# Banded attention of layer 1: the scaling of the probabilities on GpSimd, the results out of PSUM on VectorE

## What is computed

```python
def swa_sink_attention(q, k, v, sinks):
    ...
    s = jnp.einsum('bnqkgd,bnskd->bnkgqs', qc, kb).astype(F32) * (dh ** -0.5)
    s = jnp.where(valid[None, :, None, None, None, :], s, -jnp.inf)
    sink = jnp.broadcast_to(sinks.astype(F32).reshape(hk, grp)[None, None, :, :, None, None], s.shape[:-1] + (1,))
    p = jax.nn.softmax(jnp.concatenate([s, sink], axis=-1), axis=-1)[..., :-1]
    o = jnp.einsum('bnkgqs,bnskd->bnqkgd', p.astype(vb.dtype), vb)
```

## Time and profile before

| | |
|---|---|
| median of 3 runs | 2487.57 us (2487.36 to 2490.05) |
| profiled execution, first to last instruction | 2484.3 us |
| busy share TensorE, VectorE, ScalarE, GpSimd | 97%, 68%, 41%, 21% |
| the attention of layer 1 in it | 1681.4 to 1734.0 us |
| its 16 steps | about 3.0 us each |

### The profile page before, as it was taken

How to read it: one execution, slowest core, us unless ns; L and a number is a source line. 1 busy time by engine, 2 the same in 40 slices (tenths; PEclk the granted TensorE clock), 3 DMA queues, 4 the chain that set the end, 5 groups by cost and what they waited for, 6 DMA issues and landing times.

```text
span 2484.3 us, 33631 instructions
## 1 busy us (share of the span) xinstructions
PE 2417.9 (97%) x12846; PEld 1905.7 (77%) x12846; DVE 1688.6 (68%) x2659; ACT 1029.0 (41%) x1810; POOL 523.9 (21%) x485
## 2 busy tenths in 40 slices
PE   9999999998999999999999999998999999999998
PEld 6587778875556878888888886775878888888887
DVE  5389966855654698777765478728579777775557
ACT  5423324545444343333333344529344333333344
POOL 5025534320000023433341000000003433432000
PEclk9999989999999999999999999999999999999999
DMA  6121100010003425544568651110335544548663
GB/s 192 47 68 43 43 26 11 2 36 1 1 26 118 144 94 182 173 162 162 170 234 286 194 163 51 43 43 18 94 127 171 177 158 156 174 159 313 214 198 128
DMA packets 236271, 298.26 MB, mean 120 GB/s; under 512 B 13424, under 2 KB 175232, under 8 KB 227024
## 3 DMA queue, kind: packets, MB, share of 16 engines
q1 hardware_dynamic: 220848, 207.66, 27.1%
q0 software_dynamic: 15264, 88.45, 9.5%
HBM read 206.95 MB, written 88.60 MB: 119 GB/s over the span
## 4 chain that ended last, share of the span: by engine, by line
PE 89%; DVE 6%; ACT 3%; issue 2%; POOL 0%; DVEq 0%; ACTq 0%; POOLq 0%
PE ps L374 24%; PE ps L376 24%; PE ps L375 24%; PE ps L3084 3%; PE ps L3061 2%; PE ps L3072 1%; DVE met L2209 1%; PE ps L2448 1%; ACT d_p L1719 1%; PE ps L2462 1%; PE ps L2457 1%; PE ps L1991 1%; PE ps L2501 1%; PE ps L2425 1%; PE ps L2510 1%
## 5 line engine op out<-in xcount | busy, mean ns | idle before, releaser
L374 PE MATMUL ps<-uhi,whi 128*128 128x512 f32 x608 | 244.9, 403 | 7.9 <-DVE ulo L533 3.3
L374 PE MATMUL ps<-q_T,whi 128*128 128x512 f32 x640 | 249.2, 389 | 1.6 <-ACT upr L858 1.6
L376 PE MATMUL ps<-q_T,wlo 128*128 128x512 f32 x640 | 249.0, 389 | 0.0
L375 PE MATMUL ps<-q_T,whi 128*128 128x512 f32 x640 | 249.0, 389 | 0.0
L374 PE MATMUL ps<-q_B,whi 128*128 128x512 f32 x608 | 238.9, 393 | 2.4 <-DVE q_B L533 2.4
L374 PE MATMUL ps<-ahi,whi 128*128 128x512 f32 x616 | 240.4, 390 | 0.0
L376 PE MATMUL ps<-ahi,wlo 128*128 128x512 f32 x616 | 239.7, 389 | 0.0
L375 PE MATMUL ps<-alo,whi 128*128 128x512 f32 x616 | 239.7, 389 | 0.0
L375 PE MATMUL ps<-ulo,whi 128*128 128x512 f32 x608 | 237.0, 390 | 0.0
L376 PE MATMUL ps<-uhi,wlo 128*128 128x512 f32 x608 | 237.0, 390 | 0.0
L376 PE MATMUL ps<-q_B,wlo 128*128 128x512 f32 x608 | 236.7, 389 | 0.0
(11 more groups left out here) (474 smaller groups left out, 5161.6 us busy)
## 6 DMA issues: line engine op xcount, KB each, us to landing
wraw<-in_ffn_w_gate_dram SPq DMA_DIRECT2D x44, 512.0 KB, 5.2
wd<-in_ffn_w_down_dram POOLq DMA_DIRECT2D x22, 1024.0 KB, 7.2
w_sums<-wd POOLq DMA_DIRECT2D x22, 1024.0 KB, 5.1
wraw<-w_sums SPq DMA_DIRECT2D x40, 512.0 KB, 3.8
araw<-act_sums SPq DMA_DIRECT2D x40, 512.0 KB, 4.6
wraw<-in_ffn_w_down_dram SPq DMA_DIRECT2D x30, 512.0 KB, 5.9
araw<-acts SPq DMA_DIRECT2D x30, 512.0 KB, 6.0
wraw<-in_ab_w_in_dram SPq DMA_DIRECT2D x24, 512.0 KB, 3.8
```

Source lines behind the costliest of these rows:

```text
L374: nc.tensor.matmul(dst, wh, xh, start=start, stop=False, **kw)
L375: nc.tensor.matmul(dst, wh, xl, start=False, stop=False, **kw)
L376: return nc.tensor.matmul(dst, wl, xh, start=False, stop=stop, **kw)
```

## The change

In `norm`, the product of `d_p` with `d_inv` leaves VectorE. A new function `swa_pool`, called in GpSimd's list behind `d_prepare`, does the same product in the same place, and waits for the reciprocal (`d_den`) in each step. `result` leaves ScalarE: VectorE copies the 128x256 numbers out of PSUM, as the last piece of each step, behind `norm(n)`.

```diff
@@ swa_act
-            def result(n):
-                b, g = divmod(n, 2)
-                act.wait_ge(*after("d_out", n + 1))
-                act.activation(dq[:, 2 * g:2 * g + 2, b * P:(b + 1) * P],
-                               bank(6 + n % 2)[:, 0:256].rearrange("p (a n) -> p a n", a=2), ACT.Copy).then_inc(S("d_y"), 1)
-
             soft(0)
             for n in range(2 * NB):
                 if n + 1 < 2 * NB:
                     soft(n + 1)
                 move(n)
-                if n:
-                    result(n - 1)
-            result(2 * NB - 1)
@@ swa_dve
                 dve.reciprocal(d_inv[n % 2][:, :], d_sum[n % 2][:, :]).then_inc(S("d_den"), 1)
-                dve.wait_ge(*after("d_den", 2 * n + 2))
-                dve.tensor_tensor(d_p[:, n % 2, :, 64 + k0:256], d_p[:, n % 2, :, 64 + k0:256],
-                                  d_inv[n % 2][:, :].unsqueeze(2).broadcast_to([P, 4, 192 - k0]), ALU.mult).then_inc(S("d_p"), 1)
+
+            def result(n):
+                b, g = divmod(n, 2)
+                dve.wait_ge(*after("d_out", n + 1))
+                dve.tensor_copy(dq[:, 2 * g:2 * g + 2, b * P:(b + 1) * P],
+                                bank(6 + n % 2)[:, 0:256].rearrange("p (a n) -> p a n", a=2)).then_inc(S("d_y"), 1)
@@
                 norm(n)
+                if n:
+                    result(n - 1)
+            result(2 * NB - 1)
+
+        def swa_pool(pool):
+            for n in range(2 * NB):
+                k0 = d_keys(n // 2)
+                pool.wait_ge(*after("d_den", 2 * n + 2))
+                pool.tensor_tensor(d_p[:, n % 2, :, 64 + k0:256], d_p[:, n % 2, :, 64 + k0:256],
+                                   d_inv[n % 2][:, :].unsqueeze(2).broadcast_to([P, 4, 192 - k0]), ALU.mult).then_inc(S("d_p"), 1)
@@ gpsimd
             d_prepare(pool)
+            swa_pool(pool)
             ffn_park(pool, 1)
```

## The result

The changed kernel takes 2546.91 us (median of 4 runs, 2545.89 to 2547.97) against 2487.47 us: 59.4 us more, a ratio of 1.0234 (95% interval 1.0214 to 1.0254). The forecast was 2551.6, with a range from 2529 to 2566.

A forecast was written before the change was run, and what follows sets the result against it. The prediction took ScalarE's chain of waits to set layer 1's attention round, 3.02 us. It put +44 us on the closed circle of waits at full clock, +64 with TensorE's falling clock: 2487.57 + 64 = 2551.6 us, range 2529 to 2566.

The forecast's parts named there:

- the ring: Layer 1 attention: product, transposes, values, copy, masking and reciprocal wait in a closed circle; 6.29 us a round against 3.02.
- The links: Eight successive waits and pieces of work in one attention round, from reciprocal to next reciprocal, summing to 6.29 us.
- hand-over from GpSimd to TensorE: Between GpSimd's product and TensorE's transposes in each attention round: taken as 0.2 us.
- from masking to reciprocal's end: VectorE's stretch behind the copy in each attention round, masking's start to reciprocal's end: 1.99 us.
- The clock: TensorE's clock falls and rises again in the attention rounds, two thirds from +44 to +74: +64 us in all; 50%.
- The sum: Forecast total over the attention: +44 us at the full clock, +64 us with TensorE's clock falling and rising.
- its tail: Behind the attention's last reciprocal: slower product on GpSimd and a last hand-over from VectorE to ScalarE, +0.8 us.
- Full clock throughout: Rival: TensorE's idle gap in the attention stays too short to lower its clock; +44, 2531.6 us; 18%.
- Low throughout: Rival: TensorE's block of work in the attention never brings its clock back; +74, 2561.6 us; 18%.
- GpSimd's product wasn't dearer: Rival it answers: GpSimd's attention product takes 1.84 to 2.02 us, not 1.48; +69 to +72 us; 7%.
- The rival that the ring costs nothing: VectorE in the attention isn't held up by the copy, ScalarE's relief decides; -3 us, 2484.6; -3 to +2 together 5%.
- Its second part: In the attention, the two buffers of d_p become the next limit: 3.15 us a round, +2 us, 2489.6.

The follow-up runs named there:

- values first: The changed kernel with TensorE's values of step n - 1 put ahead of its transposes of step n: 2499.59 us.
- the run with the copy alone: The kernel before with only the result's copy moved from ScalarE to VectorE, the product left on VectorE: 2540.76 us.
- the held clock: The changed kernel with 20 small unused matmuls a step in TensorE's idle gap, between scores and transposes: 2529.94 us.
- the four buffers: The changed kernel with VectorE's copy one step later and d_p in four buffers in place of two: 2489.89 us.
- the scores earlier with four and with two buffers: The changed kernel, copy one step later, TensorE's scores one step ahead, before the values; d_p in four or two buffers: 2493.98 and 2492.77 us.
- the copy two steps later: The version with scores one step ahead and four d_p buffers, VectorE's copy put off one more step (result n - 3): 2489.19 us.
- the exponentials earlier: The version with the copy two steps later, with ScalarE's exponentials and VectorE's masking one step further ahead: 2493.61 us.
- the product alone: The changed kernel with the result's copy left on ScalarE, so only the product moves to GpSimd: 2491.69 us.

## Why the prediction held, point by point

**The mechanism** was right: every link of the ring and its order are in the trace. The waits, the chain and the three runs that cut the ring in different places (copy left on ScalarE, +4.7; copy later, +2.9; values first, +12.6) show it; the run with the copy alone shows which edit closes it.

**The links.** GpSimd's product was sized at 1.48 us; all fourteen of the full size took 1.47:

```profile
L1786 POOL TENSOR_TENSOR d_p<-d_p,d_inv 128x768 f32<-128x768 f32 x14 | 20.6, 1470 | 79.5 <-DVE d_inv L1764 79.5
L1769 DVE COPY dq<-ps 128x256 f32<-128x256 f32 x16 | 6.8, 424 | 76.0 <-PE ps L1694 76.0
```

VectorE's copy took 0.424 (forecast 0.42). The price of 1.88 us, an estimate from the Trainium skill ("GPSIMD Engine Reference", "Performance versus the Vector engine"), was too high for this form: the measured ratio to VectorE's 0.96 is 1.53, not 1.96, which that section gives for an addition of two full tensors of 2048 elements and not for a product with a held operand. Two links were too long. The hand-over from GpSimd to TensorE is 0.04 us, where I had taken 0.2 as a value between two rows; it is as short as the one from VectorE to TensorE. And from masking to reciprocal's end it is 1.87 us (1712.37 to 1714.24 in the trace after), not 1.99, since the sum starts 0.08 us behind the start of the instruction that makes the sink's exponent and not 0.18. The values took 1.06 and not 1.09. Two small errors cancel: the hand-over from the values to VectorE is 0.02 and not 0.08, and the transposes take 1.10 and not 1.03. Together that makes the ring 5.99 us where the sum said 6.29, some 4 us too much in 14 rounds.

**The clock** was sized as two thirds of the way from full to low. The trace after has rounds of 7.75 us with both links low, the held clock gives 5.99, so a fully low round costs 1.76 more, where I had said 2.1. The twelve rounds from 1692.7 to 1780.5 take 7.32 us on average: 75% of the way. The larger share met the smaller price, and the result is 16.5 to 18.6 us where the sum had 20. That these two errors cancel is luck; the share was a guess between two bounds, not derived.

The reason given for it is borne out in part. Both levels occur in the same kernel, and filling the gap keeps the clock full, so the idle gap is what lets it fall. But I had set a gap of 3.2 us against the 2.8 us ahead of the fall in the earlier trace rows, and that comparison fails. In the eleven rounds of steps 3 to 13 TensorE stood idle ahead of the transposes for only 2.28 to 3.03 us, in nine of them for less than 2.8, and the clock fell all the same. Four gaps in a row, of 2.28, 2.29, 2.28 and 2.28 us, were followed by transposes of 1.97, 1.09, 1.09 and 1.97 us. So the length of the gap doesn't say at which level the next block starts. Nor does the clock change where the work does. Behind 5.4 us of work at 0.50 (1701.40 to 1706.80) it was at 0.98 while TensorE stood idle, and it fell again in the middle of the next block (columns as in the earlier trace rows):

```profile
1706.90:1709.10 2.20, 0.00 (x0) 0.00 (x0) 0.58 (x4) 1.80 (x9) 1.47 (x1) 0.98 0.00 0
1709.15:1710.20 1.05, 1.05 (x10) 0.88 (x10) 0.00 (x0) 0.11 (x2) 0.00 (x0) 1.00 0.00 0
1710.25:1712.00 1.75, 1.75 (x10) 0.73 (x10) 0.00 (x0) 1.02 (x1) 0.00 (x0) 0.54 0.00 0
```

What decides in which round it falls stays open.

**The sum.** Forecast +44 for the ring and its tail, +20 for the clock; measured about 41 and 18. The forecast is 4.6 us too high, most of it in the links.

**The rivals.** Full clock throughout would have been 2531.6; the run with the clock held is at 2529.9, and that case didn't occur. The two agree more closely than the sum deserves, since the held run has some 2 us of lower clock in its first round; without them the links' excess shows, about 3.5 us. Low throughout didn't occur either. GpSimd's product wasn't dearer. The rival that the ring costs nothing wanted 0.7 us of slack for links of 3.96 us, and didn't come near it. Its second part, a two-buffer ring of 3.15 us once VectorE is free, was the weak place: with the ring cut the rounds were 3.25, and rings over the masking, over the scores and over the copy two steps on were found there that I hadn't listed.

**Expectations that failed** were nearly all of one kind. For the values first, the four buffers, the scores earlier with four and with two buffers, the copy two steps later and the exponentials earlier, I named the ring that I was removing and took an engine's list or a shorter ring as the next limit. Each time another ring, over three or four engines and two steps, was longer. For the product alone and the copy one step later, too, the rounds were 3.26 and 3.25 us where I had 3.1.

**A product beside VectorE's masking.** In the changed kernel VectorE stands still while GpSimd multiplies, so nothing could be seen of the two in each other's way. In the version with the copy two steps later they do overlap: the product runs from 1713.38 to 1714.85 and maskings start at 1714.07, 1714.35 and 1714.63, and the product keeps its 1.47 us:

```profile
1713.38 1.47 POOL L1791 TENSOR_TENSOR d_p<-d_p,d_inv 128x768 f32<-128x768 f32 x1 [1.64 <-DVE d_inv L1767]
...
1714.07 0.35 DVE L1748 CUSTOM_DVE_ANT_0 d_s<-ps,band 128x192 f32<-128x192 f32 x1
```

The masking reads one operand from PSUM and one from SBUF. The Trainium skill ("SBUF — State Buffer", "Who interferes with whom") says that a VectorE instruction with at most one SBUF input, outside its two-port modes, doesn't contend with GpSimd; this trace agrees, where the earlier trace rows with two SBUF inputs showed a stretched pair.

## What to carry to other kernels

When a piece of work moves to another engine, don't ask first how busy that engine is; ask what stands behind the new wait in its list, and follow from there who is waited for in turn. If the walk comes back to the same wait of the next step, the round is the sum of the links, however idle all engines are. If it comes back only some steps later, divide the sum by the number of steps; the longest such quotient, or the longest engine's list, sets the round. Putting the copy one step later took 56 of 59 us off in this way, and every later trial ended at a ring that had not been walked. A round stretched in this way can also leave TensorE idle long enough for its clock to fall, which is charged on top: here 18 us on 41.

## What the runs showed of the hardware that I hadn't expected

- Matmuls whose results nobody uses, put into the gap, made the kernel 16.5 us faster (59.4 to 42.9 us above the kernel before) with the granted clock at 1.00 from the third round on.
- The granted clock rose while TensorE stood idle and fell while it worked (0.98 from 1706.90 to 1709.10, 0.54 from 1710.25 to 1712.00), and gaps of the same 2.28 us were followed by transposes at either level.
- In the closed ring the lower clock costs more than the product on GpSimd does: 16.5 us with the product there and 19 with it on VectorE, against 8.1 (clock held) and 5.6 (clock free) for the product.
- GpSimd hands over to TensorE as quickly as VectorE does, 0.04 us in the chain of waits, while its own next instruction that waits for it comes 0.30 us later.
